# Cutting each half of 528 columns at 256 instead of 264, and laying it over two PSUM banks without a gap

## What is computed

```python
def mixer_c(h, past_c, w_in, conv_w, w_out):
    z = h @ w_in
    bg, cg, hx = jnp.split(z, 3, axis=-1)
    hc, new_past_c = causal_dwconv(cg * hx, past_c, conv_w)
    return (bg * hc) @ w_out, new_past_c

def conv_ffn(h, past_f, w_up, conv_w, w_down):
    z = h @ w_up
    g, up = jnp.split(z, 2, axis=-1)
    gc, new_past_f = causal_dwconv(g, past_f, conv_w)
    return (jax.nn.silu(gc) * up) @ w_down, new_past_f

def trunk(...):
    for l in range(DEPTH):          # DEPTH = 2
        h = rmsnorm(x, norm_mix[l])
        ... # l = 0: mixer_ab, l = 1: mixer_c
        x = x + y
        h = rmsnorm(x, norm_ffn[l])
        y, pf = conv_ffn(h, past_f[l], w_up[l], conv_f_w[l], w_down[l])
        x = x + y
    return rmsnorm(x, norm_final), ...
```

## Time and profile before

| | us |
|---|---|
| median of 3 runs | 2107.96 |
| lowest and highest run | 2106.73, 2108.14 |
| span of the profiled execution | 2104.3 |
| PE busy in it | 2088.9 (99%) |
| DVE, POOL, ACT busy | 1528.3, 960.8, 743.6 |

### The profile page before, as it was taken

How to read it: one execution, slowest core, us unless ns; L and a number is a source line. 1 busy time by engine, 2 the same in 40 slices (tenths; PEclk the granted TensorE clock), 3 DMA queues, 4 the chain that set the end, 5 groups by cost and what they waited for, 6 DMA issues and landing times.

```text
span 2104.3 us, 36430 instructions
## 1 busy us (share of the span) xinstructions
PE 2088.9 (99%) x15402; PEld 2079.5 (99%) x15402; DVE 1528.3 (73%) x1863; ACT 743.6 (35%) x1143; POOL 960.8 (46%) x601
## 2 busy tenths in 40 slices
PE   9999999999999999999999999999999999999998
PEld 9999999999999999999999999999999999999997
DVE  6999679867666666666997677798666666766667
ACT  6564255332222232223633222453322233222234
POOL 4756435543434434434465344445344344444444
PEclk9999999999999999999999999999999999999999
DMA  4101311111111111111111111111111111011112
GB/s 166 51 31 42 125 61 41 61 43 40 61 41 61 53 49 41 52 51 51 51 41 61 41 61 41 51 51 52 47 43 51 51 61 51 31 61 41 61 43 83
DMA packets 34322, 115.38 MB, mean 55 GB/s; under 512 B 3888, under 2 KB 7472, under 8 KB 34160
## 3 DMA queue, kind: packets, MB, share of 16 engines
q1 hardware_dynamic: 34016, 112.52, 15.9%
q10 hardware_dynamic: 144, 0.54, 0.1%
HBM read 108.42 MB, written 4.62 MB: 54 GB/s over the span
## 4 chain that ended last, share of the span: by engine, by line
PE 98%; POOL 0%; ACT 0%; DMA 0%; DVE 0%; issue 0%; SPq 0%; POOLq 0%; DVEq 0%
PE psum L659 32%; PE psum L661 32%; PE psum L660 32%; PE psum L760 1%; DMA x<-x_t 0%; PE psum L705 0%; PE psum L780 0%; PE psum L716 0%; POOL x L1254 0%; SPq L590 0%; DVE work L1790 0%; POOL w_lo L1106 0%; PE psum L798 0%; ACT xs_hi L1298 0%; POOL w_lo L1211 0%
## 5 line engine op out<-in xcount | busy, mean ns | idle before, releaser
L659 PE MATMUL psum<-xs_hi,w_hi 128*128 128x264 f32 (+2 forms) x3784 | 1101.5, 291 | 2.8 <-DVE xs_lo L1750 0.6
L661 PE MATMUL psum<-xs_hi,w_lo 128*128 128x264 f32 (+2 forms) x3784 | 1100.1, 291 | 0.0
L660 PE MATMUL psum<-xs_lo,w_hi 128*128 128x264 f32 (+2 forms) x3784 | 1096.6, 290 | 0.0
L1106 POOL TENSOR_TENSOR w_lo<-raw,w_hi 128x512 fp32r<-128x512 f32 (+1 forms) x412 | 665.6, 1628 | 824.8 <-ACT w_hi L1293 740.0
L659 PEld LDWEIGHTS psum<-xs_hi,w_hi 128*128 128x128 f32 x3784 | 712.0, 188 | 5.4 <-issue 1.5
L661 PEld LDWEIGHTS psum<-xs_hi,w_lo 128*128 128x128 f32 x3784 | 711.4, 188 | 0.0
L660 PEld LDWEIGHTS psum<-xs_lo,w_hi 128*128 128x128 f32 x3784 | 711.4, 188 | 0.0
L659 PE MATMUL psum<-act_hi,w_hi 128*128 128x352 f32 x1200 | 388.5, 324 | 0.1
L661 PE MATMUL psum<-act_hi,w_lo 128*128 128x352 f32 x1200 | 388.2, 324 | 0.0
L660 PE MATMUL psum<-act_lo,w_hi 128*128 128x352 f32 x1200 | 385.5, 321 | 0.0
L1293 ACT ACTIVATE w_hi<-raw 128x512 fp32r<-128x512 f32 x383 | 234.0, 625 | 289.8 <-PE psum L661 269.0
(11 more groups left out here) (229 smaller groups left out, 1943.8 us busy)
## 6 DMA issues: line engine op xcount, KB each, us to landing
raw<-slabs SPq DMA_DIRECT2D x186, 512.0 KB, 3.2
x<-x_t SPq DMA_DIRECT2D x15, 528.0 KB, 6.5
y_t<-x SPq DMA_DIRECT2D x6, 400.0 KB, 3.0
raw<-slabs SPq DMA_DIRECT2D x4, 256.0 KB, 8.1
y_t<-x SPq DMA_DIRECT2D x1, 600.0 KB, 3.0
x<-x_t ACTq DMA_DIRECT2D x1, 528.0 KB, 4.9
x<-mix SPq DMA_DIRECT2D x1, 512.0 KB, 3.2
y_t<-x SPq DMA_DIRECT2D x1, 512.0 KB, 3.8
```

Of the source, the lines that this page charges most:

```text
L659: nc.tensor.matmul(out, w_hi[:, w], hi, start=start, stop=False, skip_group_check=reopen)
L660: nc.tensor.matmul(out, w_hi[:, w], lo, start=False, stop=False, skip_group_check=reopen)
L661: return nc.tensor.matmul(out, w_lo[:, w], hi, start=False, stop=stop, skip_group_check=reopen)
L1106: nc.gpsimd.tensor_tensor(w_lo[:, slab], src, w_hi[:, slab].bitcast(F32), ALU.subtract).then_inc(weights_ready, 1)
```

## The change

The cut of a half moves from column 264 to column 256: `PART` becomes 264 rounded down to a multiple of `LINE` = 16 columns (64 bytes), and the two parts have 256 and 272 columns. The first part is now written to the last 256 columns of the first bank and the second to the first 272 of the next, so that the 528 results lie in one contiguous stretch. ACT and DVE read the stretch as one run (`half_of`), and where there were three instructions for the two prompt pieces and the sample there are two. The 32 columns of `rms_spread`'s rest move from column 300 of `Y_BANK` to column 0. The number of matmuls and the number of columns streamed stay the same.

```diff
-PART = HALF // 2
+LINE = 16
+PART = HALF // 2 // LINE * LINE
+PARTS = ((0, PART), (PART, HALF))
+BANK = 512
...
-        def halves_of(bank):
-            return psum[:, bank:bank + 2, 0:PART]
-
-        def two(ap):
-            return ap.rearrange("p (c n) -> p c n", c=2)
+        def part_of(bank, h):
+
+            return psum[:, bank, BANK - PART:BANK] if h == 0 else psum[:, bank + 1, 0:HALF - PART]
+
+        def half_of(bank, first=0, end=HALF):
+
+            both = psum[:, bank:bank + 2, :].rearrange("p a b -> p (a b)")
+            return both[:, BANK - PART + first:BANK - PART + end]
...
+            def part_cols(kp, which, h):
+                at = kp * KP_COLS + which
+                return slice(at + PARTS[h][0], at + PARTS[h][1])
+
             def block_product(slab, which, first_bank, kp, opens, closes, reopen=False):
 
                 for h in range(2):
-                    at = kp * KP_COLS + which + h * PART
-                    last = split_product(psum[:, first_bank + h, 0:PART], tile_at(slab, kp), xs_hi[:, at:at + PART],
-                                         xs_lo[:, at:at + PART], opens, closes, reopen=reopen)
+                    cols = part_cols(kp, which, h)
+                    last = split_product(part_of(first_bank, h), tile_at(slab, kp), xs_hi[:, cols], xs_lo[:, cols],
+                                         opens, closes, reopen=reopen)
                 return last
...
-                rms_spread(p, psum[:, Y_BANK, 300:300 + ROW_REST])
+                rms_spread(p, psum[:, Y_BANK, 0:ROW_REST])
...
-                nc.scalar.activation(two(g[:, 2:2 + HALF]), halves_of(X_BANKS[0]), ACT.Copy).then_inc(part_copied, 1)
-                at = 2 + HALF
-                nc.scalar.activation(g[:, at:at + PART], psum[:, Y_BANK, 0:PART], ACT.Copy)
-                nc.scalar.activation(g[:, at + PART:2 + SEQ], psum[:, Y_BANK + 1, 0:split],
+                nc.scalar.activation(g[:, 2:2 + HALF], half_of(X_BANKS[0]), ACT.Copy).then_inc(part_copied, 1)
+                nc.scalar.activation(g[:, 2 + HALF:2 + SEQ], half_of(Y_BANK, 0, HALF_PROMPT),
                                      ACT.Copy).then_inc(part_copied, 1)
...
-                dve.tensor_tensor(g[:, at:at + PART], psum[:, x_bank, 0:PART], r_rows[:, HALF:HALF + PART], ALU.mult)
-                dve.tensor_tensor(g[:, at + PART:2 + SEQ], psum[:, x_bank + 1, 0:split],
-                                  r_rows[:, HALF + PART:SEQ], ALU.mult)
-                dve.tensor_tensor(g[:, 2 + SAMPLE + GAP:2 + GAP_COLS], psum[:, x_bank + 1, split:PART],
+                dve.tensor_tensor(g[:, 2 + HALF:2 + SEQ], half_of(x_bank, 0, HALF_PROMPT), r_rows[:, HALF:SEQ],
+                                  ALU.mult)
+                dve.tensor_tensor(g[:, 2 + SAMPLE + GAP:2 + GAP_COLS], half_of(x_bank, HALF_PROMPT),
                                   r_rows[:, SAMPLE:COLS], ALU.mult).then_inc(tile_evacuated, 1)
```

More of the change, by code:

```diff
@@ L866, in group @@
                     for kp in range(KP):
-                        at = kp * KP_COLS + which + h * PART
-                        last = split_product(psum[:, first_bank + h, 0:PART], tile_at(slab, kp),
-                                             xs_hi[:, at:at + PART], xs_lo[:, at:at + PART],
-                                             opens and kp == 0, kp == KP - 1, reopen=not opens)
+                        cols = part_cols(kp, which, h)
+                        last = split_product(part_of(first_bank, h), tile_at(slab, kp), xs_hi[:, cols],
+                                             xs_lo[:, cols], opens and kp == 0, kp == KP - 1, reopen=not opens)
                 return last
@@ L1508, in first_pair @@
                 g = conv_in
[L1509 removed]
                 act.wait_ge(tile_done, group_done(p, 0, 0, GATE_DONE))
                 act.wait_ge(squares_summed, DVE_SUMS * (p + 1))
[L1512 to L1515 removed]
+                nc.scalar.activation(g[:, 2:2 + HALF], half_of(X_BANKS[0]), ACT.Copy).then_inc(part_copied, 1)
+                nc.scalar.activation(g[:, 2 + HALF:2 + SEQ], half_of(Y_BANK, 0, HALF_PROMPT),
                                      ACT.Copy).then_inc(part_copied, 1)
[L1517 removed]
+                nc.scalar.activation(g[:, 2 + SAMPLE + GAP:2 + GAP_COLS], half_of(Y_BANK, HALF_PROMPT),
                                      ACT.Copy).then_inc(part_copied, 1)
@@ L1524, in first_pair @@
                                      ACT.Copy).then_inc(r_ready, 1)
-                nc.scalar.activation(r_rows[:, 1024:COLS], psum[:, Y_BANK, 300:300 + ROW_REST],
+                nc.scalar.activation(r_rows[:, 1024:COLS], psum[:, Y_BANK, 0:ROW_REST],
                                      ACT.Copy).then_inc(r_ready, 1)
@@ L1589, in pair @@
                 p1 = first_p1 if before == FIRST else half(up, 1)
-                nc.scalar.activation(two(p1), halves_of(x_bank), ACT.Copy).then_inc(part_copied, 1)
+                nc.scalar.activation(p1, half_of(x_bank), ACT.Copy).then_inc(part_copied, 1)
                 entry_hi(p, b, q, 4)
@@ L1601, in copy_u2 @@
                         act.wait_ge(c_gated, 1)
-                    nc.scalar.activation(two(half(up, 0)), halves_of(x_bank), ACT.Copy).then_inc(part_copied, 1)
+                    nc.scalar.activation(half(up, 0), half_of(x_bank), ACT.Copy).then_inc(part_copied, 1)
                 third = p != 2 and (b, q) == (1, 0)
@@ L1619, in pair @@
                     act.wait_ge(tile_evacuated, pair_read(p, unit, C11_READ))
-                nc.scalar.activation(two(half(up, 1)), halves_of(Z_BANK), ACT.Copy).then_inc(part_copied, 1)
+                nc.scalar.activation(half(up, 1), half_of(Z_BANK), ACT.Copy).then_inc(part_copied, 1)
                 if p != 2 and q == 0 and b == 1:
@@ L2147, in first_pair @@
                 for i, bank in enumerate((Z_BANK, X_BANKS[0])):
-                    dve.tensor_tensor(two(half(prod[0], i)), halves_of(bank), two(half(r_rows[:], i)),
+                    dve.tensor_tensor(half(prod[0], i), half_of(bank), half(r_rows[:], i),
                                       ALU.mult).then_inc(tile_evacuated, 1)
@@ L2272, in c11 @@
                     p1 = first_p1 if before == FIRST else half(up, 1)
-                    dve.tensor_tensor(two(g0), halves_of(Y_BANK), two(p1), ALU.add).then_inc(tile_evacuated, 1)
+                    dve.tensor_tensor(g0, half_of(Y_BANK), p1, ALU.add).then_inc(tile_evacuated, 1)
                     dve.wait_ge(tile_evacuated, pair_read(p, unit, C11_READ))
@@ L2279, in c22 @@
                     dve.wait_ge(part_copied, 3 * n + 3)
-                    dve.tensor_tensor(two(half(up, 1)), halves_of(x_bank), two(half(up, 1)),
+                    dve.tensor_tensor(half(up, 1), half_of(x_bank), half(up, 1),
                                       ALU.add).then_inc(tile_evacuated, 1)
@@ L2284, in c21 @@
                     dve.wait_ge(tile_done, group_done(p, b, q, 5))
-                    dve.tensor_tensor(two(half(up, 0)), halves_of(Z_BANK), two(half(up, 0)),
+                    dve.tensor_tensor(half(up, 0), half_of(Z_BANK), half(up, 0),
                                       ALU.add).then_inc(tile_evacuated, 1)
```

4 lines of the change are left out of this document (removed).

## The result

The changed kernel takes 2113.31 us (median of 6 runs, 2112.24 to 2114.27) against 2106.78 us of the kernel before (6 runs, 2106.54 to 2108.14): ratio 1.0028, 95% interval 1.0018 to 1.0037. It is slower by 6.5 us, where 13.3 us less (2094.7 us) had been forecast. The profiled span is 2110.9 us against 2104.3. That execution took 2112.99 us, so 2.1 us lie around the program; the 3.7 us given above set a median against the span of another execution. The forecast difference doesn't hang on it.

What follows compares the result with a forecast made beforehand. PE's own stream was taken to bound the kernel; 4740 pairs at 240.5 instead of 243.3 ns, 2.8 ns less each, give 13.3 us off 2107.96, so 2094.7 us, range 2089 to 2109; everything else counted as nothing.

Steps and rivals of the forecast that it cites:

- What bounds the kernel: Whole kernel: PE, busy 99% of the span, sets the end; pair-unit changes count by the distance between matmul starts.
- The term for 256: First parts in pair units: 256 columns at 116.6 ns, the last chunk's pace, where 264 took 121.64.
- The term for 272: Second parts in pair units: 272 columns at 123.9 ns, from the line through 256 and 352; bounds 123.3 to 125.3.
- The second sign: Pair units before: second parts, starting mid-line, some 0.9 ns a matmul slower than first parts, credited to that start.
- The bounds: Pair units: gain per pair between 1.4 ns (6.6 us) and 3.4 ns (16 us), unless 256 ran in dearer surroundings.
- PSUM, ACT, DVE, what is late next: Around the pair units: PSUM offset free, joined DVE read about 664 ns, path gain 0 to 0.4 us, nothing becomes late.
- A dear rhythm: Pair units: 256 and 272 fall into 352's dearer rhythm, 2.15 ns a matmul, 20.4 us over forecast, 2115.1 us; chance 0.11.
- Columns only: Pair units: alignment doesn't matter, 256 + 272 keeps 2 x 11.6 ns excess; no change, 2107.96 us; chance 0.18.
- Only the start counts: Pair units: only second parts improve, by 0.9 ns, 4.3 us in all, 2103.7 us; chance 0.15.
- The chances: Whole kernel's time: faster 0.64, same (2103.7 to 2112.2 us) 0.27, slower 0.09.
- The rule weighed in the prediction: Pair units: columns over 2.4 GHz plus some 2.5 ns whatever the alignment, so 256 + 272 costs as 264 + 264, 2107.96 us.

Runs made afterwards that it cites:

- m1_table: Kernel's computation left out; PE streams blocks of 48 matmuls, one size and start (or walk of four starts) each; 256 columns took 113.7 to 119.9 ns a matmul.
- v_cont264: The changed kernel with parts back at 264 and 264, keeping new PSUM placement and joined evacuations; 2107.95 us, ratio 1.0002 against the kernel before.
- v_cut240: The changed kernel with parts of 240 and 288 columns in place of 256 and 272; 2105.38 us, ratio 0.9992 against the kernel before.
- v_lo16: The changed kernel with only the operand's low part (xs_lo) moved 64 bytes, 16 columns, further; 2110.42 us, ratio 1.0013 against the kernel before.
- v_cut272: The changed kernel with the long part first, 272 then 256 columns; 2104.11 us, ratio 0.9987 against the kernel before.
- v_cut280: The changed kernel with parts of 280 and 248 columns, the second starting off a 16-column line; 2100.40 us, ratio 0.9969 against the kernel before.
- v_extra144: The kernel before with one superfluous 144-column matmul at the head of each of the 21 down units; 2103.58 us, ratio 0.9982.

## Why the prediction was wrong, step by step

- **What bounds the kernel**: right. PE is the path, its pace decides, and the starts in the timeline, not the durations, measure it. 4740 pairs times the change of the pair gives 6.6 us, as much as the spans differ.
- **The term for 256 failed.** I took 116.6 ns from the 36 matmuls of the last chunk and called it "its own row". It is a row of 256 columns at two other starts. In the pair units the four starts give 118.5. That is 1.9 ns x 4740 = 9.2 us.
- **The term for 272 failed.** 123.9 ns came from a straight line through 256 and 352; it measures 126.1, above the upper bound of 125.3 too. That is 2.2 ns x 4740 = 10.4 us. The line had no meaning: one size alone spreads by 6.2 ns over starts (m1_table), and I was after 1.4 ns.
- **The two terms together** are 19.6 us, which leads from -13.3 to the +6.6 measured, but for 0.3 us of rounding; nothing else moved.
- **The second sign misled.** First parts are 0.8 ns cheaper than second parts in the kernel before (121.23 against 122.02 in the means), so the difference is real, though two rows that are good to 0.01 us in 12 matmuls (0.8 ns each) couldn't show it. I put it down to the start in the middle of a line. The buffer moved by 8 columns swaps the two, so it does come from the starts; but with `kp` steps of 3712 columns the parts in mid-line are the cheaper ones (121.25 against 122.0), and 280 + 248 is as good as any cut. Lines are not the measure.
- **The bounds** were wrong in kind. The note that 256 might be "in dearer surroundings than its 36 matmuls" named what happened, but gave it no number; the two paces of 352 were there to give one.
- **PSUM, ACT, DVE, what is late next**: right. v_cont264 prices them all at 0.0 ns a pair, and its time is the same within 0.1%; the joined DVE instruction takes 668 ns where 664 was put.
- **The rivals.** *A dear rhythm* (2115.1 us, slower) came nearest to the 2113.3 measured: its price of 2.15 ns a matmul on top of the forecast stands beside the 1.9 and 2.2 measured, its group "over 2.93 us" beside 2.93. Its reason, that what 352 shows between two places can happen to 256 and 272, holds; its other support, the weight load, doesn't (240 columns keep 112.1 ns in v_cut240). What it lacked is that in the pair units the operand's starts take part in the pace (v_lo16). *Columns only* (no change) is closest to what isolation shows, 244.1 against 243.8, but not to the kernel. *Only the start counts* falls: second parts were to lose 0.9 ns beyond their columns, and went up by 4.1 ns for 8 columns that are 3.3 ns at 2.4 GHz.
- **The chances.** 0.09 for slower was too little. The argument against the rival was again the 116.6 ns of the earlier trace rows, so one row carried the forecast and also spoke against its rival.

The rule weighed in the prediction, from the Trainium skill, "TensorE: Matmul & The Clock Gate", section "Back-to-back issue gap", gives the distance of isolated matmuls by columns alone, and says itself that in a stream with weight loads both set it. For 256 columns it gives 109.2 ns; the runs here have 113.7 to 119.9 for them, by start, so for this stream neither its size nor the columns alone are borne out.

## What to carry to other kernels

Where PE is busy 99% and a change alters matmul sizes by a few columns, price it only with rows of the same size, the same set of operand starts and the same neighbours; a row of the same size from another loop can be off by as much as the whole gain sought. If there is no such row, the spread of one size over places (here 158.9 to 161.1 ns for 352) is a bound to start from, on both sides, and even that was too narrow here: the term for 272 was off by 2.2 ns. And look at the units behind the changed one: here they held more (7.0 us) than the changed units did.

## What the runs showed of the hardware

- For 256 columns the distance of starts ranges from 113.7 to 119.9 ns with the start of the moving operand alone (eight starts, 8 columns apart), for 272 from 123.5 to 126.7, for 264 from 120.1 to 126.6, at a granted clock of 1.00 (2.4 GHz). Moving the low part by 64 bytes takes a pair from 244.64 to 243.28 ns.
- In the kernels and the replayed streams a long run of equal matmuls holds one of a few paces, 158.9, 160.0 or 161.1 ns for 352 columns, to its last matmul, after a dozen or two at another one in some cases; what comes right before the run selects it: the size of the last part (v_cut272, v_cut280), or one matmul of 144 columns, with which the kernel does more and ends 3.7 us earlier (v_extra144). The first mixer's run of 430 takes each of the three in one kernel or another though nothing ahead of it was changed (158.9 before, 160.0 in v_cut280, 161.1 in v_extra144). That is up to 1 us by itself, so a profile of one execution can't price a change there.
- Several blocks of one size and one start stand near multiples of 6.67 ns, the time of 16 columns at 2.4 GHz: 119.9 (256), 126.6 (264), 126.7 (272), 146.7 (320), 160.0 (352), 180.1 (400). More than half of the blocks don't (113.7 and 118.5 for 256, for instance).
- Below 240 columns the distance hardly falls any more: 118.5 ns for 256, 112.1 for 240, 111.0 for 224, each with its weight load.
- The offset of the output in its PSUM bank, and reading one stretch over two banks rather than two runs, cost nothing that the kernels can tell (243.25 ns a pair either way). One isolated block differs: 264 columns at start 0 took 121.5 ns into column 0 and 120.2 into column 248.

What stays open is the mechanism. The runs show that size, start and entry select the pace, not what in the read of the operand does it. 256 at one start went at 113.7 in one block and at 117.8 in another with the same start modulo 64 columns, and a unit with one start for all halves took 120.55 ns where 118.3 was expected, so no run here lets the pace of a new cut be worked out beforehand. The layout with halves 576 columns apart was not tried in the kernel: it would need 10.7 KB more of each partition, and some 500 bytes are free.
